# A two-layer decoder trunk on one core: an early exponent table, row maxima moved ahead, weight loads held, two more weight splits on Pool, and the gating mask a stage earlier

## The chip, the cores and the metric

The kernel runs on one core of a Trainium2 chip. That core has five engines that run side by side and meet only at semaphores: TensorE (PE, matrix multiplies and transposes), VectorE (DVE), ScalarE (ACT), GpSimd (POOL) and SyncE (SP, which here only starts transfers). The metric is device time in microseconds (us) of one launch; lower is better. Semaphore `hi_ready`, for instance, is a counter that ACT raises and that other engines wait on.

## The reference, cut to what matters

The program computes a decoder trunk of two layers on 256 positions of width 1024, all in float32. Each layer has three sub-blocks:

```
x = x + 1/2 * SwiGLU_a(RMSNorm(x))        # 1024 -> 2816 -> 1024
x = x + Mixer(RMSNorm(x))
x = x + 1/2 * SwiGLU_b(RMSNorm(x))
# layer 0 mixer: softmax attention (8 heads) beside a gated delta rule (8 heads), one output projection
# layer 1 mixer: u, v = gelu(h @ w_in); v = RMSNorm per group; gate = tril(w_s) @ v + b_s; (u*gate) @ w_out
```

In the delta rule the sequence is cut into four chunks of 64. Within a chunk a triangular system is solved; across chunks a state of 64 x 64 per head is carried (the scan): `v_new = u - w @ state`, `o = q_dec @ state + attn @ v_new`, `state = state * decay + k_tail^T @ v_new`. Its result is normalized per head (`rms_norm(o)`), multiplied with `silu(z)`, put beside the attention result, and goes through the output projection.

## The kernel before

The program is one straight list of instructions for each engine, written out by hand. It goes through six stages in order: feed-forward 0, the attention and delta-rule mixer ("the mixer", `ab`), feed-forward 1, feed-forward 2, the spatial gating mixer (`sg`), feed-forward 3. On each engine the order of the code is the order of execution; nothing reorders it, and an engine that waits holds up all that is behind it.

**Weights** come in units of 1 MB (128 partitions x 2048 words). `load_unit` on SP copies unit j into slot j mod 4 of the ring `raw`, once the slot's former unit has been split. The split makes two reduced-precision parts of a float32 weight: ACT copies `raw` to `whi` (`hi`, L466), and `wlo = raw - whi` is made by DVE (`lo`, L889) or by POOL (`pool_lo`, L426). `POOL_LO` lists the units that POOL splits; before the change these are units 12 to 15 of the mixer, its output projection. ACT may overwrite a slot of `whi` only when PE is done with the unit that is four before it (`unit_done`). PE multiplies with both parts, three products for each tile.

**The softmax part of the mixer.** ACT ends the short convolutions with `conv_silu(5)` (Silu table), then copies transposed channels out (`nt_out(5)`), then runs `exps(h)` for each head h, which needs the table of the exponential. `exps(h)` waits for `row_max(h)` on DVE (L1139 to L1141: the maximum over a row of scores, and the bias made of it), and PE transposes the exponentials (L1766) and computes the scores of head h + 2 (L1666) behind them. On DVE, between the first maxima, stand the head sums and the inverse root of the delta rule's q and k (`head_sums(1)` L1126, `rsqrt` L866 to L875, `head_norm` L1153), the copies of the summed log decays (L1161 and L1162, semaphore `gc_ready`) and the decay differences (`Dec`, L1184 and L1186), whose exponential ACT makes at L720 before it goes on to copy transposed heads (L686).

**The scan and what is behind it.** SP waits for `w_sums` 1, which PE raises when half of the matrices w are there, ahead of the scan, and then issues four loads, units 16 to 19 of the mixer's numbering, the first four of feed-forward 1. The scan is n = 0 to 3: DVE copies (L1265), PE L1918, L1924, L1906, L1910. Behind it DVE normalizes the result (`o_weighted` L1257 and L1259, `rsqrt`, and two products L1286 that raise `y_gdn`), while PE multiplies the attention half of the output projection (24 products, L1337 to L1339, `for t: for kk`). PE then waits for `y_gdn` 2, transposes (`y_transposes`, L1805) and goes on with the rest (`down`). ACT copies the transposes (`yT_hi`, L732), and splits units 16 and 17; DVE does `yT_lo` (L1222), its half of the split of units 16 and 17 (L889), and then updates X (`x_update`, L939, semaphore `x_updated`, four for each stage).

**The start of a stage** (`next_x`, `row_norm`, `spread_diag`): DVE computes 1 / rms of each row (`rsqrt`), multiplies it into an identity (L956, `r_diag`), and PE spreads it with two small products (L1480, `r_sums`) between its first weight products.

**The gating stage.** POOL waits for `x_updated` 16, the end of feed-forward 2, loads `v_norm_row` (1 MB, one row copied to all partitions) and `ws_raw` (the gating matrices, 512 KB), both through its own queue (L377), and multiplies `ws_raw` with a triangle (L450, `ws_masked`). PE transposes the result (L1972), ACT copies it to `wsT` (L826, `wsT_ready`) behind its splits. DVE waits for both loads (`sg_loaded` 32) before it scales v (L1309, `v_ready`), and splits two more units behind that; PE computes the first gates (L1958) when `v_ready` has reached 4.

Of the kernel before, what the change touches and what calls it, by code (L numbers as in the profile page):

```python
# [5 lines left out]
P = 128  # L6
D_MODEL, SEQ, D_FF = 1024, 256, 2816
NT = SEQ // P
# [5 lines left out]
HEADS = 8  # L14
# [59 lines left out]
def build_trunk(nc, x, positions, norm_w, w_gate, w_up, w_down, ab_in, q_norm, w_q_b, kv_norm, w_kv_b,  # L74
# [57 lines left out]
    u_ab = ab_units()  # L132
# [14 lines left out]
    with ctx:  # L147
# [5 lines left out]
        def S(name):  # L153
            if name not in sems:
                sems[name] = ctx.enter_context(nc.semaphore(name))
            return sems[name]
# [64 lines left out]
        v_norm_row = at(R0 + 2048, SGW)  # L221
        ws_raw = at(0, GROUPS, P)

# [87 lines left out]
        DT_SEED_BANKS = ((3, 6), (5, 2))  # L311
        POOL_LO = [u_ab + 12, u_ab + 13, u_ab + 14, u_ab + 15]
        SG_BANK = [(4, 5), (4, 5), (0, 1), (2, 3)]
# [5 lines left out]
        def _(sp_):  # L319
# [38 lines left out]
            if stop_after not in ("ffn0", "ab"):  # L358
                sp_.wait_ge(S("w_sums"), 1)
                ffn_loads(u_ffn[1])  # L360
                ffn_loads(u_ffn[2])
                for j in range(u_sg, u_sg + 24):
                    load_unit(j)
                ffn_loads(u_ffn[3])
# [10 lines left out]
        def _(pool):  # L375
            def load(dst, src, name):
                pool.dma_start(dst, src).then_inc(S(name), 16)  # L377
# [62 lines left out]
            pool_lo(u_ab + 14)  # L440
            pool_lo(u_ab + 15)

            if stop_after == "ab":
                return

            pool.wait_ge(S("x_updated"), 16)
            load(v_norm_row, bc(sg_norm, [P, SGW]), "sg_loaded")
            load(ws_raw, sg_ws[0].rearrange("g i j -> i g j"), "sg_loaded")
            pool.wait_ge(S("sg_loaded"), 32)
            nc.gpsimd.tensor_tensor(ws_raw, ws_raw, bc(const("tril128").unsqueeze(1), [P, GROUPS, P]),  # L450
                                    ALU.mult).then_inc(S("ws_masked"), 1)


        @block.scalar
        def _(act):
# [213 lines left out]
            conv_silu(5)  # L669
            nt_out(5)  # L670

# [16 lines left out]

            exps(0)
            exps(1)  # L690
            for h in range(HEADS):
# [85 lines left out]
            for n in range(4):  # L777
# [5 lines left out]
                if n >= 2:  # L783
                    o_squares(n - 2)
            yT_hi(4, 8)
            for j in range(16, 18):
                hi(b + j)
            next_x(2)
# [64 lines left out]
        def _(dve):  # L853
# [290 lines left out]
            row_max(0)  # L1144
            row_max(1)
            head_sums(1)
            dve.wait_ge(S("head_sums"), 2)
            both = qk_head_ss.rearrange("p a m -> p (a m)")
# [6 lines left out]
            head_norm(QKVn[1], 1, 1.0).then_inc(S("k_normed"), 1)  # L1155
            row_max(2)
            gcf, ekf = (a.rearrange("p t h -> p (t h)") for a in (gc, ek))
            dve.wait_ge(S("gc_sums"), 2)
            for c in range(2):
                r = slice(64 * c, 64 * c + 64)  # L1160
                link(nc.vector.tensor_copy(gcf[r, :], B[2 + c][r, 0:16]))  # L1161
                ins = TT(ekf[r, :], B[2 + c][r, 16:32], gcf[r, :], ALU.subtract)  # L1162
                if c == 0:
                    link(ins)
            ins.then_inc(S("gc_ready"), 1)

            m3 = lambda a: a.rearrange("p (m j) -> p m j", j=64)
# [7 lines left out]
            for h in range(HEADS):  # L1175
                if 0 < h < HEADS - 2:
                    row_max(h + 2)
# [109 lines left out]
            yT_lo(4, 8)  # L1287
            for j in range(16, 18):
                lo(b + j)
            next_x(2, [1.0, 1.0])  # L1290
# [42 lines left out]
        def _(pe):  # L1333
# [595 lines left out]
            pe.wait_ge(S("o_weighted"), 2)  # L1929
            for t in range(NT):  # L1930
                for kk in range(4):
                    wh, wl = slot(b + 12 + kk // 2)
# [81 lines left out]
```

## Time and profile before

| | us |
|---|---|
| median of 3 runs | 1094.08 |
| lowest, highest | 1093.31, 1097.67 |
| the profiled execution's own time | 1093.22 |
| its span (first to last instruction) | 1091.2 |
| outside the span (launch and end) | 2.0 |

| engine | busy us | share of span |
|---|---|---|
| PE | 1065.9 | 98% |
| DVE | 637.0 | 58% |
| ACT | 514.2 | 47% |
| POOL | 49.8 | 5% |

The mean granted TensorE clock is 0.998 of full speed. An engine's busy share says how much of the span it worked; a row of the timeline gives start, length, engine, line, operation, the tiles written and read and their shapes, and in square brackets the time that the engine sat idle just before, with the instruction that ended the wait. The chain of waits is the profile's own walk back from the last instruction to what released each step.

### The profile page before, as it was taken

How to read it: one execution, taken by the hardware profiler on the slowest of the kernel's cores; microseconds unless marked ns; L12 is line 12 of the kernel's file. 1: busy time of each engine (PE TensorE's matmuls, PEld its weight loads, DVE VectorE, ACT ScalarE, POOL GpSimd, SP SyncE). 2: the span in 40 equal slices, each digit the busy share in tenths (PEclk: the TensorE clock that was granted, in tenths of full speed). 3: DMA queues.
4: the chain of work that ended last, by engine and by line, in shares of the span. 5: the costliest groups of instructions: out<-in, count | busy, mean ns of one | idle time of the engine just before them, and what ended most of it. 6: DMA issues, size and time to landing. Idle time of an engine off the chain costs nothing.

```text
span 1091.2 us, 18956 instructions
## 1 busy us (share of the span) xinstructions
PE 1065.9 (98%) x8393; PEld 969.9 (89%) x8393; DVE 637.0 (58%) x783; ACT 514.2 (47%) x619; POOL 49.8 (5%) x32
## 2 busy tenths in 40 slices
PE   7999999999888999999999999999999999999998
PEld 7999988998777799998889999887788889999986
DVE  5756543699753675555457655435665547555542
ACT  6644433585673454443345444334665436444430
POOL 1000000110172000000000000001000000000000
PEclk9999999999999999999999999999999999999999
DMA  9856555253005276655538555554554465655531
GB/s 311 268 184 191 193 191 175 92 196 117 2 4 157 78 232 193 193 183 177 184 113 254 178 188 192 194 182 149 192 173 172 165 221 187 187 176 187 191 115 39
DMA packets 127194, 184.88 MB, mean 169 GB/s; under 512 B 4205, under 2 KB 101722, under 8 KB 126986
## 3 DMA queue, kind: packets, MB, share of 16 engines
q1 hardware_dynamic: 126368, 181.85, 51.3%
q0 software_dynamic: 448, 1.71, 0.5%
q8 instruction: 66, 1.08, 0.4%
q10 hardware_dynamic: 298, 0.12, 0.1%
q14 instruction: 14, 0.11, 0.0%
HBM read 182.62 MB, written 1.05 MB: 168 GB/s over the span
## 4 chain that ended last, share of the span: by engine, by line
PE 92%; DVE 4%; issue 2%; ACT 1%; DMA 0%; POOLq 0%; ACTq 0%; POOL 0%; DVEq 0%
PE banks L1337 21%; PE banks L1338 20%; PE banks L1339 20%; PE banks L1378 7%; PE banks L1382 7%; PE banks L1379 7%; PE banks L1735 1%; PE banks L1461 1%; PE banks L1462 1%; PE banks L1463 1%; PE banks L1425 1%; PE banks L1958 1%; DVE wlo L889 1%; DVE arena L1209 1%; DMA pos_rows<-in_positions 0%
## 5 line engine op out<-in xcount | busy, mean ns | idle before, releaser
L889 DVE TENSOR_TENSOR wlo<-raw,whi 128x2048 fp32r<-128x2048 f32 (+1 forms) x167 | 383.4, 2302 | 228.1 <-ACT whi L466 228.0
L466 ACT ACTIVATE whi<-raw 128x2048 fp32r<-128x2048 f32 (+1 forms) x171 | 324.1, 1908 | 382.0 <-PE banks L1339 241.8
L1337 PE MATMUL banks<-xTh,whi 128*128 128x256 f32 x1408 | 397.4, 282 | 1.0 <-DVE wlo L1011 0.9
L1338 PE MATMUL banks<-xTl,whi 128*128 128x256 f32 x1408 | 396.5, 282 | 0.0
L1339 PE MATMUL banks<-xTh,wlo 128*128 128x256 f32 x1408 | 396.5, 282 | 0.0
L1337 PEld LDWEIGHTS banks<-xTh,whi 128*128 128x128 f32 x1408 | 266.2, 189 | 1.7 <-issue 1.3
L1338 PEld LDWEIGHTS banks<-xTl,whi 128*128 128x128 f32 x1408 | 266.3, 189 | 0.0
L1339 PEld LDWEIGHTS banks<-xTh,wlo 128*128 128x128 f32 x1408 | 266.3, 189 | 0.0
L1378 PE MATMUL banks<-whi,hTh 128*128 128x512 f32 x336 | 133.4, 397 | 0.0
L1379 PE MATMUL banks<-wlo,hTh 128*128 128x512 f32 x336 | 132.3, 394 | 0.0
L1382 PE MATMUL banks<-whi,hTl 128*128 128x512 f32 x336 | 105.5, 395 | 0.0
L1378 PEld LDWEIGHTS banks<-whi,hTh 128*128 128x128 f32 x336 | 63.0, 188 | 15.5
L1382 PEld LDWEIGHTS banks<-whi,hTl 128*128 128x128 f32 x336 | 63.0, 187 | 15.4
L1379 PEld LDWEIGHTS banks<-wlo,hTh 128*128 128x128 f32 x336 | 63.0, 187 | 14.9
L1337 PE MATMUL banks<-whi,xTh 128*128 128x512 f32 (+1 forms) x160 | 64.0, 400 | 0.0
L1338 PE MATMUL banks<-wlo,xTh 128*128 128x512 f32 (+1 forms) x160 | 62.7, 392 | 0.0
L1339 PE MATMUL banks<-whi,xTl 128*128 128x512 f32 (+1 forms) x160 | 62.6, 391 | 0.0
L924 DVE TENSOR_TENSOR arena<-banks,arena 128x512 f32<-128x512 f32 x44 | 30.4, 690 | 53.6 <-PE banks L1339 53.6
L1337 PE MATMUL banks<-whi,hTh 128*128 128x512 f32 (+1 forms) x120 | 49.3, 411 | 0.0
L1339 PE MATMUL banks<-whi,hTl 128*128 128x512 f32 (+1 forms) x120 | 46.9, 391 | 0.0
L1338 PE MATMUL banks<-wlo,hTh 128*128 128x512 f32 (+1 forms) x120 | 46.9, 391 | 0.0
L915 DVE TENSOR_TENSOR arena<-banks,arena 128x512 f32<-128x512 f32 x44 | 30.3, 690 | 26.9 <-PE banks L1339 26.9
(249 smaller groups left out, 988.9 us busy)
## 6 DMA issues: line engine op xcount, KB each, us to landing
raw<-in_ffn_w_up SPq DMA_DIRECT2D x44, 1024.0 KB, 5.6
raw<-in_ffn_w_down SPq DMA_DIRECT2D x44, 1024.0 KB, 4.9
raw<-in_ffn_w_gate SPq DMA_DIRECT2D x43, 1024.0 KB, 5.4
raw<-in_sg_w_in SPq DMA_DIRECT2D x16, 1024.0 KB, 5.5
raw<-in_ab_w_in SPq DMA_DIRECT2D x8, 1024.0 KB, 5.2
raw<-in_sg_w_out SPq DMA_DIRECT2D x8, 1024.0 KB, 5.2
raw<-in_ab_w_out SPq DMA_DIRECT2D x4, 1024.0 KB, 4.8
raw<-in_ab_w_in SPq DMA_DIRECT2D x2, 832.0 KB, 4.4
```

What stands on the lines that cost most here:

```text
L466: A(whi[:, j % SLOTS, 0:kt * width], raw[:, j % SLOTS, 0:kt * width], ACT.Copy).then_inc(S("hi_ready"), 1)
L889: TT(wlo[:, j % SLOTS, 0:n], raw[:, j % SLOTS, 0:n], whi[:, j % SLOTS, 0:n].bitcast(f32), ALU.subtract).then_inc(S("lo_ready"), 1)
L915: TT(gate[:, c % 2, :].rearrange("p (b n) -> p b n", n=SEQ), B[PAIR_BANK[c][0]][:].rearrange("p (b n) -> p b n", n=SEQ), bc(r_row.unsqueez ...
L924: TT(prod[:, c % 2, :], B[PAIR_BANK[c][1]][:], gate[:, c % 2, :], ALU.mult).then_inc(S("prod_ready"), 1)
L1209: TT(LT_LEVEL[n][t].rearrange("p (m j) -> p m j", j=64), h3(LT, t), eight(f"level{LEVELS[n]}"), ALU.mult).then_inc(S("lt_level"), 1)
L1337: mm(out_ap, lh, rh, start=first, stop=False)
L1338: mm(out_ap, lh, rl, start=False, stop=False)
L1339: return mm(out_ap, ll, rh, start=False, stop=last)
L1378: mm(o, hTh[:, kk, tok], wh[:, k, c], start=kk == 0, stop=False)
L1379: mm(o, hTh[:, kk, tok], wl[:, k, c], start=False, stop=False)
L1382: last = mm(o, hTl[:, kk, tok], wh[:, k, c], start=False, stop=False)
L1425: last = transpose(B[X_BANK[k // 2]][:, 256 * (k % 2) + P * t:256 * (k % 2) + P * t + P], X[:, t, P * k:P * k + P], ident)
```

## The change

It has seven edits. One tiny exponential is put behind `conv_silu(5)`, and `nt_out(5)` moves behind `exps(0)`. On DVE the copies of the log decays and the maximum of head 2 move ahead of the inverse root, and the maximum of head 3 moves to just behind the norm of k. SP waits for `o_sums` 2, raised by PE in scan step n = 1, before the loads of feed-forward 1. Units 16 and 17 are split by POOL in place of DVE, ACT's part of unit 16 moves ahead of the last `yT_hi`, and PE's 24 products behind the scan run `for kk: for t`, so that unit 12 is released at half. The gating matrices are loaded and masked when `x_updated` reaches 8 (the end of the mixer), into another place of the arena (`R0 + 2912`); `v_norm_row` overlaps that place, and its load now waits for `wsT_ready` 2 as well.

```diff
-        ws_raw = at(0, GROUPS, P)
+        ws_raw = at(R0 + 2912, GROUPS, P)
...
-        POOL_LO = [u_ab + 12, u_ab + 13, u_ab + 14, u_ab + 15]
+        POOL_LO = [u_ab + i for i in range(12, 18)]
...
-                sp_.wait_ge(S("w_sums"), 1)
+                sp_.wait_ge(S("o_sums"), 2)
...
             pool_lo(u_ab + 15)
+            pool_lo(u_ab + 16)
+            pool_lo(u_ab + 17)
...
-            pool.wait_ge(S("x_updated"), 16)
-            load(v_norm_row, bc(sg_norm, [P, SGW]), "sg_loaded")
+            pool.wait_ge(S("x_updated"), 8)
             load(ws_raw, sg_ws[0].rearrange("g i j -> i g j"), "sg_loaded")
-            pool.wait_ge(S("sg_loaded"), 32)
+            pool.wait_ge(S("sg_loaded"), 16)
             nc.gpsimd.tensor_tensor(ws_raw, ws_raw, bc(const("tril128").unsqueeze(1), [P, GROUPS, P]),
                                     ALU.mult).then_inc(S("ws_masked"), 1)
+            pool.wait_ge(S("x_updated"), 16)
+            pool.wait_ge(S("wsT_ready"), 2)
+            load(v_norm_row, bc(sg_norm, [P, SGW]), "sg_loaded")
...
             conv_silu(5)
-            nt_out(5)
+            A(rope_tmp[:, 0, 0, 0:1], ones128[:, 0:1], ACT.Exp).then_inc(S("gate_exps"), 1)
...
             exps(0)
+            nt_out(5)
             exps(1)
...
+            hi(b + 16)
             yT_hi(4, 8)
-            for j in range(16, 18):
-                hi(b + j)
+            hi(b + 17)
...
             row_max(1)
-            head_sums(1)
-            dve.wait_ge(S("head_sums"), 2)
-            both = qk_head_ss.rearrange("p a m -> p (a m)")
-            link(rsqrt(both, both, 2 * M, 1.0))
...
-            head_norm(QKVn[1], 1, 1.0).then_inc(S("k_normed"), 1)
-            row_max(2)
             gcf, ekf = (a.rearrange("p t h -> p (t h)") for a in (gc, ek))
             dve.wait_ge(S("gc_sums"), 2)
...
             ins.then_inc(S("gc_ready"), 1)
+            head_sums(1)
+            row_max(2)
+            dve.wait_ge(S("head_sums"), 2)
+            both = qk_head_ss.rearrange("p a m -> p (a m)")
+            link(rsqrt(both, both, 2 * M, 1.0))
...
+            head_norm(QKVn[1], 1, 1.0).then_inc(S("k_normed"), 1)
+            row_max(3)
...
-                if 0 < h < HEADS - 2:
+                if 1 < h < HEADS - 2:
                     row_max(h + 2)
...
             yT_lo(4, 8)
-            for j in range(16, 18):
-                lo(b + j)
...
-            for t in range(NT):
-                for kk in range(4):
+            for kk in range(4):
+                for t in range(NT):
```

Two places show how the order on the engines moves. DVE in the softmax part of the mixer before, from the maximum of head 1 on; `banks` are the matmul results, `small` the small tiles, `128x3` the three maxima of a head:

```order
L1139 TENSOR_REDUCE small<-banks 128x3
L1140 TENSOR_TENSOR small<-small 128x1
L1141 TENSOR_TENSOR small<-small 128x2
L1126 TENSOR_REDUCE small<-arena 128x16
L866 TENSOR_SCALAR small<-small 128x32
```

And the same stretch of DVE after the change, where L1144 to L1146 are the maximum, L1155 and L1156 the copies of the decays, L1131 the head sums and L871 the first of the inverse root:

```order
L1144 TENSOR_REDUCE small<-banks 128x3
L1145 TENSOR_TENSOR small<-small 128x1
L1146 TENSOR_TENSOR small<-small 128x2
L1155 COPY small<-banks 64x16
L1156 TENSOR_TENSOR small<-banks,small 64x16
L1155 COPY small<-banks 64x16
L1156 TENSOR_TENSOR small<-banks,small 64x16
L1131 TENSOR_REDUCE small<-arena 128x16
L1144 TENSOR_REDUCE small<-banks 128x3
L1145 TENSOR_TENSOR small<-small 128x1
L1146 TENSOR_TENSOR small<-small 128x2
L871 TENSOR_SCALAR small<-small 128x32
```

Four copies and the third maximum stand ahead of the inverse root; all of them stood behind it. POOL from its splits to the end of its list before:

```order
L426 TENSOR_TENSOR wlo<-raw,whi 128x2048 x2
L377 DMA arena<-in_sg_v_norm 128x2048
L377 DMA arena<-in_sg_w_s 128x8x128
L450 TENSOR_TENSOR arena<-arena,C 128x1024
L147 UNCONDITIONAL_BRANCH
```

And after:

```order
L426 TENSOR_TENSOR wlo<-raw,whi 128x2048 x4
L377 DMA arena<-in_sg_w_s 128x8x128
L451 TENSOR_TENSOR arena<-arena,C 128x1024
L377 DMA arena<-in_sg_v_norm 128x2048
L147 UNCONDITIONAL_BRANCH
```

Two splits are added behind the two that were there, and the load of `v_norm_row` goes from the head of the gating's part to its end. ACT around the end of the scan, before and then after (first the squares of the scan's result, then `yT_hi`, with the splits `whi<-raw`):

```order
L773 ACTIVATE arena<-banks 128x4x64 x2
L732 ACTIVATE hTh<-banks 128x256 x4
L466 ACTIVATE whi<-raw 128x2048 x2
L481 ACTIVATE arena,small<-X 128x512 x2
```

```order
L778 ACTIVATE arena<-banks 128x4x64 x2
L470 ACTIVATE whi<-raw 128x2048
L737 ACTIVATE hTh<-banks 128x256 x4
L470 ACTIVATE whi<-raw 128x2048
L485 ACTIVATE arena,small<-X 128x512 x2
```

One of the two splits has moved ahead of the four copies.

## Rows read from the trace of the kernel before

**Rows 1.** Timeline of PE and ACT at the first exponentials (start us, us, engine, line).

```profile
279.19 0.55 PE L1766 MATMUL banks<-C,arena 128*128 128x128 f32 x3 [3.10 <-ACT arena L680]
276.74 1.28 ACT L678 ACT_TABLE_LOAD   x1
```

**Rows 2.** Stretch: us; busy us of PE, PEld, DVE, ACT, POOL; clock; DMA.

```profile
274.64:287.66 13.02, 9.41 (x73) 7.31 (x72) 11.96 (x35) 9.07 (x28) 0.00 (x0) 1.00 0.00 0
```

**Rows 3.** Timeline of ACT at the decay exponential.

```profile
287.70 1.06 ACT L720 ACTIVATE arena<-arena 128x1024 f32<-128x1024 f32 x1 [0.97 <-DVE arena L1186]
```

**Rows 4.** Chain of waits in order of time, the scan (start us, us, what).

```profile
344.31 1.44 issue
```

**Rows 5.** Timeline of DVE's copies in the scan, and of SP's loads.

```profile
340.38 0.42 DVE L1265 COPY arena<-banks 64x256 f32<-64x256 f32 x1 [6.24 <-PE banks L1893]
342.94 0.43 DVE L1265 COPY arena<-banks 64x256 f32<-64x256 f32 x1 [0.78 <-PE banks L1906]
347.91 0.41 DVE L1265 COPY arena<-banks 64x256 f32<-64x256 f32 x1 [3.19 <-PE banks L1906]
336.90 0.37 SPq L343 DMA_DIRECT2D raw<-in_ffn_w_gate  x1
```

**Rows 6.** Stretch in the scan, columns as in rows 2.

```profile
346.00:349.00 3.00, 3.00 (x56) 3.00 (x56) 0.75 (x2) 0.92 (x3) 0.00 (x0) 0.50 1.10 349
```

**Rows 7.** Timeline of PE, ACT and DVE behind the scan.

```profile
355.14 0.39 PE L1339 MATMUL banks<-whi,hTl 128*128 128x512 f32 x1
367.32 0.66 PE L1425 MATMUL banks<-C,X 128*128 128x128 f32 x4 [1.83 <-DVE X L939]
360.19 3.74 ACT L466 ACTIVATE whi<-raw 128x2048 fp32r<-128x2048 f32 x2
357.08 1.29 DVE L1286 TENSOR_TENSOR arena<-arena,small 128x512 f32<-128x512 f32 x2
362.17 4.49 DVE L889 TENSOR_TENSOR wlo<-raw,whi 128x2048 fp32r<-128x2048 f32 x2 [0.93 <-ACT whi L466]
```

**Rows 8.** Timeline of POOL, and of DVE beside it.

```profile
292.48 1.90 POOL L393 TENSOR_TENSOR arena<-arena,small 128x1024 f32<-128x1024 f32 x1
324.67 9.09 POOL L426 TENSOR_TENSOR wlo<-raw,whi 128x2048 fp32r<-128x2048 f32 x2
760.00 4.47 POOL L450 TENSOR_TENSOR arena<-arena,C 128x1024 f32<-128x1024 f32 x1 [5.47 <-DMA arena<-in_sg_w_s]
292.57 1.83 DVE L1141 TENSOR_TENSOR small<-small 128x2 f32<-128x2 f32 x1
```

**Rows 9.** Line L889 from 759 to 767 us: ns least/median/most, starts.

```profile
L889 DVE TENSOR_TENSOR wlo<-raw,whi x2: 2285/3376/4468, 760.0 to 762.2; 128x2048 fp32r<-128x2048 f32 x2
```

**Rows 10.** Timeline of DVE and PE at the start of feed-forward 1.

```profile
374.47 0.69 DVE L939 SCALAR_TENSOR_TENSOR X<-banks,X 128x512 f32<-128x512 f32 x1 [0.91 <-PE banks L1339]
379.98 0.15 DVE L900 TENSOR_TENSOR small<-small 128x2 f32<-128x2 f32 x1
382.60 0.48 DVE L956 TENSOR_SCALAR arena<-C,small 128x128 f32<-128x128 f32 x2
383.22 0.63 PE L1480 MATMUL banks<-arena,C 128*128 128x128 f32 x4
```

**Rows 11.** Timeline of PE, ACT and DVE in the gating stage.

```profile
764.53 1.09 PE L1972 MATMUL banks<-C,arena 128*128 128x128 f32 x8 [0.95 <-POOL arena L450]
776.66 1.89 PE L1958 MATMUL banks<-arena 128*128 128x256 f32 x8
770.14 1.05 ACT L826 ACTIVATE arena<-banks 128x512 f32<-128x512 f32 x2
769.13 1.67 DVE L1309 SCALAR_TENSOR_TENSOR arena<-arena,small 128x256 f32<-128x256 f32 x4
```

**Rows 12.** DMA issues on POOL's queue: KB each, us from issue to landing.

```profile
arena<-in_sg_v_norm POOLq DMA_DIRECT2D x1, 1024.0 KB, 5.3
arena<-in_sg_w_s POOLq DMA_DIRECT2D x1, 512.0 KB, 6.3
```

More of the change, by code:

```diff
@@ L1145, in _ @@
             row_max(1)
-            head_sums(1)
-            dve.wait_ge(S("head_sums"), 2)
-            both = qk_head_ss.rearrange("p a m -> p (a m)")
-            link(rsqrt(both, both, 2 * M, 1.0))
-            def head_norm(a, i, scale):
-                a3 = a.rearrange("p t (h d) -> p (t h) d", d=DK)
-                return STT(a3, a3, scale, bc(qk_head_ss[:, i, :].unsqueeze(2), [P, M, DK]), ALU.mult, ALU.mult)
-            head_norm(QKVn[1], 1, 1.0).then_inc(S("k_normed"), 1)
-            row_max(2)
             gcf, ekf = (a.rearrange("p t h -> p (t h)") for a in (gc, ek))
@@ L1165, in _, with head_norm @@
             ins.then_inc(S("gc_ready"), 1)
+            head_sums(1)
[3 more added lines that the diff above has]
+            link(rsqrt(both, both, 2 * M, 1.0))
+            def head_norm(a, i, scale):
+                a3 = a.rearrange("p t (h d) -> p (t h) d", d=DK)
+                return STT(a3, a3, scale, bc(qk_head_ss[:, i, :].unsqueeze(2), [P, M, DK]), ALU.mult, ALU.mult)
+            head_norm(QKVn[1], 1, 1.0).then_inc(S("k_normed"), 1)
+            row_max(3)
             m3 = lambda a: a.rearrange("p (m j) -> p m j", j=64)
```

## The prediction, made before the changed kernel had run

> **What bounds the kernel now.** PE works for 98% of the span, so a change can only gain where PE waits, or lose by making it wait. I read the chain of waits first, for the stretches that are not PE's; then the timeline of each engine around the edits; then the stretches, for the clock and for how full an engine is; last the transfers of POOL's queue. Five places matter, and all but the first are short:
>
> 1. Before the first exponentials PE sits idle 3.10 us, and a table load of 1.28 us on ACT lies in that wait [rows 1].
> 2. In the scan PE issues nothing for 1.44 us that any other engine explains [rows 4], and from 346 to 349 us its granted clock is 0.50, the 1.2 GHz level of the two [rows 6]. SP has started four weight loads at 336.90 [rows 5], and in the half-clock stretch DMA moves 349 GB/s [rows 6].
> 3. Behind the output projection PE waits 1.83 us for DVE's update of X [rows 7], and DVE has spent 4.49 us on the splits of units 16 and 17 just ahead of it [rows 7].
> 4. At the start of feed-forward 1 PE's spreading product stands at 383.22, right behind DVE's r_diag, which ends at 382.60 + 0.48 = 383.08 [rows 10]. There is 0.1 us of slack.
> 5. In the gating stage PE waits 0.95 us for POOL's mask [rows 11].
>
> **Exponent table and maxima: 0.** By themselves they let the first exponentials start when the first bias is ready, at about 275.6 and no longer at 278.04 (the end of the table load at 276.74 + 1.28), so PE's first transposes come some 2.3 us earlier. The question is what is late next. DVE is full from the first maximum to the decay differences: 11.96 us busy of 13.02 [rows 2], the rest being the small gaps between its chained instructions, and ACT waits at the end of that stretch for DVE's last one before it can make the decay exponential [rows 3]; ACT copies the transposed heads behind that, and PE needs these. The change moves DVE's work about inside this stretch: first maxima, four copies, head sums, third maximum, inverse root, norm, fourth maximum, norm, differences. The set is the same as before. So the decay exponential starts at 287.7 as before, PE waits behind it and not at 276, and 2.3 us go into another wait. I check that the third maximum doesn't stall DVE: the scores of head 2 are a few products behind the transposes, which would start at 276.8 and take 0.55 [rows 1]; I estimate them at 278.7, and DVE, with its copies and sums done first, arrives at about 278.6. Bounds: -2.3 us (all of it reaches the end), +0.5 (a short stall of DVE); I take 0, by the full engine.
>
> **Loads held to mid-scan: -2.8.** Scan step n = 0 takes 342.94 - 340.38 = 2.56 us, step n = 1 takes 347.91 - 342.94 = 4.97 [rows 5]. Without the stall it should be as short as its neighbour: 2.41 gained, in which the 1.44 and the first slow microseconds lie. The slow clock goes on for another microsecond behind 347.91 [rows 6]; I take 0.4 for it, from 1.1 us of matmuls at half rate, of which about a third is on the path. The cause that I assume is that PE's instructions are fetched by the same DMA engines, which were full. The loads now start at about 344.6, when the instructions for the rest of the scan are there, and the next block is wanted only behind 24 long products. Unit 16 is needed at 352.7 (new time), some 8 us after the issue; in rows of this trace a load of 1 MB lands 5.3 us after issue on POOL's queue [rows 12], so that it should be there. Bounds: -3.2, and 0 if the stall only moves to a later step.
>
> **Units 16 and 17 off DVE: -1.85 and +4.6.** Taking 4.49 us off DVE lets it update X when PE has finished the quarter, so that PE's wait of 1.83 us goes [rows 7]. The units themselves are not urgent: PE's spreading product at 383.22 [rows 10] stands amid its first products with units 16 and 17, 16 us behind that update, and one split takes POOL 9.09 / 2 = 4.54 us [rows 8].
>
> But POOL and DVE get into each other's way. At 292.57 a DVE product of two numbers per partition, from small tiles, took 1.83 us, and ended at 294.40; POOL's product, started at 292.48, ended at 294.38 [rows 8]. At 760.00 POOL's mask and DVE's splits ran together: DVE's two took 2285 and 4468 ns, POOL's 4.47 us [rows 8, 9]. The second DVE split, started at 762.2, ended at 766.7, and the only reading that fits all three is DVE 2.28, POOL 2.2, DVE 2.2, each alone: who waits gets the port when the other's instruction ends, even when the other has a next one ready. The Trainium skill's page "SBUF — State Buffer" (Who interferes with whom) says the same of a DVE instruction with two SBUF inputs beside a GpSimd one that reads SBUF, that one of them fully blocks, and not for one with a PSUM input. By that rule, the trace agrees.
>
> Now where POOL's split of unit 16 falls. ACT may start its part when PE has released unit 12. With `for kk: for t` that is the end of the twelfth product behind the scan, which in the old trace is the one at 355.14 with 0.39 us [rows 7]: 355.53. ACT takes 3.74 / 2, some 1.85 us: 357.4. POOL asks at 357.45. DVE at that time is in the first of the two products that end the norm, 357.08 to 357.72, with the second to follow [rows 7]; both read two SBUF operands. POOL gets in between, holds for 4.54 us, and the second product, which raises `y_gdn`, ends at 357.75 + 4.54 + 0.69 = 363.0 where it ended at 358.37. PE's transposes, all of them, wait for it: +4.6. The margin is 0.3 us, both chains start from the same last product of the scan and move together. Bounds: 0 (the request comes behind the second product), +5.3 (it comes ahead of both and the whole split stands in front). The split of unit 17 comes behind `yT_hi` and meets only updates with a PSUM input: nothing.
>
> **Mask a stage earlier: +1.9 at feed-forward 1.** `x_updated` 8 is the end of the update at 374.47 + 0.69 = 375.16 [rows 10]; POOL issues the load at about 375.4. It lands 6.3 us after issue when it stands behind the 1 MB load [rows 12]; alone, half as large, I put it at 4.3 (bounds 3 and 6.3). Then POOL's mask, 2.2 us without company (4.47 less DVE's 2.28 [rows 8, 9]), stands at 379.8 to 382.0. DVE's norm chain begins at 379.98 [rows 10] with products of two small tiles, the kind that was held at 292.57. It is held 1.0 to 2.2 us over the bounds of the landing, I take 2.0, and with 0.1 us of slack at place 4 PE waits 1.9. A landing within 2 us or behind 7.5 us would cost nothing.
>
> **Gating stage: +2.1.** The wait of 0.95 goes. But `v_norm_row` is now loaded only behind the copies to `wsT`, which end at 770.14 + 1.05 = 771.2 [rows 11], and takes 5.3 us [rows 12]: 776.6. DVE would have scaled v at 769.13 [rows 11]; it now starts at 776.6, and ends 1.67 us later, at 778.3. PE wants to start the gates at 776.66 at the latest [rows 11], 0.95 earlier without its former wait, and starts at 778.3: 1.65 later than before. Behind the gates (until 780.1) it wants unit b + 4 of the stage, and DVE's split of it, queued behind the scaling, ends at 778.3 + 2.25 = 780.5: 0.45 more. Later units have room. Bounds: 1.2 (landing 0.9 us faster, as no other load is under way) to 2.7.
>
> **Sum.** -2.8 - 1.85 + 4.6 + 1.9 + 2.1 = +3.95 us. The profiled execution took 1093.22 us (span 1091.2 and 2.0 around it): 1097.2. The median of the runs shown is 0.9 above it: 1098.0. I put 1097.6 between the two. What a measurement of this kernel can tell from no change is about 0.5%, 5.5 us: slower begins at 1099.6, faster at 1088.6.
>
> **Rivals.**
> - *POOL misses the norm's second product* (DVE keeps the port, or ACT's split ends 0.4 us later). For it: the margin of 0.3 us. Against: the pattern at 760. It takes away 4.6: 1093.
> - *The clock falls behind the long idle stretches: slower.* The forecast makes two long waits, 4.6 us before the transposes and some 2.6 us before the gates. The half-clock stretch of the old scan followed a wait of 1.44 us [rows 4, 6], against it stands that behind 3.10 us idle [rows 1] the clock stayed at 1.00 over the next 8 us [rows 2]. If it falls in the dense products behind both waits, and each time for as long as at 346 to 349, half of 3 us is lost twice: +3, 1100.6. It decides once both idle stretches lower the clock. The page "TensorE: Matmul & The Clock Gate" of the Trainium skill (Part 1) states that idleness takes the clock to the lower level; the trace shows one case for it and one against.
> - *The front gain reaches the end* (PE and ACT, not DVE, set the pace of the softmax part). For it: 3.10 us of PE idle. Against: rows 2 and 3. It gives -2.3: 1095.3.
> - *The mask runs clear of the norm.* For it: the landing of a lone 512 KB load is not in the trace. It gives -1.9: 1095.7.
>
> **Chances.** The forecast 0.44, POOL misses 0.18, clock 0.18, front gain 0.10, mask clear 0.10. Slower by over 0.5% holds most of the clock case (0.13) and the upper tail of the forecast (0.09): 0.22. Faster by over 0.5% needs three of the rivals together or a scan that gains more than I see: 0.09. The rest, 0.69, is within. The range goes from POOL missing, less 1.5, to the clock case: 1091.5 to 1101.
>
> **What will show it.** The first exponential should start near 275.7, and the decay exponential still near 287.7. Scan step n = 1 should take about 2.6 us and the clock there should read 1.00. The second of the two products L1291 should read about 5.2 us, and PE's wait before its transposes 4.7. The wait of 1.83 should be gone. POOL's mask should stand on DVE's inverse root of feed-forward 1, and PE wait about 1.9 us before `r_sums`. DVE should wait some 7 us for `v_norm_row`, PE about 2.6 before the first gates. I am wrong if the second product reads 0.69, if the decay exponential moves 2 us ahead, or if the stall of the scan comes back a step later.

## The result and the profile after

The changed kernel takes 1101.79 us (median of 14 runs, 1098.07 to 1104.32), the kernel before 1094.03 us beside it (14 runs, 1092.70 to 1100.66). The ratio is 1.0057, with a 95% interval of 1.0041 to 1.0072: slower by about 6.2 us, where the forecast had 1097.6, some 3.5 to 4 us above the kernel before. By the ratio, on the 1094.08 that the forecast started from, this is 1100.3, inside its range up to 1101; the median of 1101.79 itself lies above that range. Two executions behind this document (3689.89 us of the kernel before, 1491.17 us of the variant with the filler products) stand far outside all others and are left out of the ratios. The profiled execution took 1103.21 us (span 1101.4), 10.2 more in the span than the one of before.

I read the waits of PE first: it is busy for 97% of the span, so a loss must be a wait of PE or work of PE that takes longer. From the profile after, from 270 to 800 us (engine, line, what it waits for; us in total, times, longest):

```profile
PE banks L1808 <- DVE arena L1291: 4.4, 1, 4.4
PE banks L1961 <- DVE arena L1312: 3.2, 1, 3.2
PE banks L1703 <- ACT arena L690: 3.0, 1, 3.0
PE banks L1483 <- DVE arena L961: 2.0, 1, 2.0
```

Of before, the long ones were 3.10 at the first exponentials and 1.83 for X [rows 1, 7]. The four above stand where the forecast had put them. Then I went through the places. At the first exponentials, after, the timeline of ACT (start us, us, engine, line):

```profile
273.58 1.28 ACT L674 ACT_TABLE_LOAD   x1
275.56 0.46 ACT L682 ACTIVATE arena<-banks,small 128x128 f32<-128x128 f32 x1 [0.49 <-DVE small L1146]
287.51 1.06 ACT L725 ACTIVATE arena<-arena 128x1024 f32<-128x1024 f32 x1 [2.09 <-DVE arena L1191]
```

and of PE:

```profile
276.71 0.55 PE L1769 MATMUL banks<-C,arena 128*128 128x128 f32 x3 [0.69 <-ACT arena L684]
289.19 1.08 PE L1703 MATMUL banks<-C,arena 128*128 128x128 f32 x4 [3.00 <-ACT arena L690]
```

The table load lies ahead of the first maximum now, and PE's first transposes come 2.5 us earlier than in [rows 1]. But the decay exponential stands at 287.51, where it was at 287.70 [rows 3], and PE waits 3.00 us behind it in place of 3.10 ahead of it. The scan, DVE's copies:

```profile
342.04 0.42 DVE L1270 COPY arena<-banks 64x256 f32<-64x256 f32 x1 [6.23 <-PE banks L1896]
344.60 0.43 DVE L1270 COPY arena<-banks 64x256 f32<-64x256 f32 x1 [0.78 <-PE banks L1909]
347.17 0.42 DVE L1270 COPY arena<-banks 64x256 f32<-64x256 f32 x1 [0.78 <-PE banks L1909]
349.72 0.43 DVE L1270 COPY arena<-banks 64x256 f32<-64x256 f32 x1 [0.78 <-PE banks L1909]
```

Every step takes 2.56 us. The one of 4.97 in [rows 5] is gone, and with it the issue gap of [rows 4] (a stretch in which PE waits for nothing that the profile shows). Behind the scan, the timeline of ACT, DVE, POOL and PE:

```profile
354.50 1.91 ACT L470 ACTIVATE whi<-raw 128x2048 fp32r<-128x2048 f32 x1 [2.39 <-PE banks L1342]
355.95 5.60 DVE L1291 TENSOR_TENSOR arena<-arena,small 128x512 f32<-128x512 f32 x2
356.49 4.52 POOL L426 TENSOR_TENSOR wlo<-raw,whi 128x2048 fp32r<-128x2048 f32 x1 [20.78 <-ACT whi L470]
361.61 1.97 PE L1808 MATMUL banks<-C,arena 128*128 128x128 f32 x8 [4.41 <-DVE arena L1291]
370.37 0.60 PE L1428 MATMUL banks<-C,X 128*128 128x128 f32 x4
```

POOL's split starts in the first of DVE's two products, and the pair takes 5.60 us where it took 1.29 [rows 7]; the wait of 1.83 us for X has gone from the last row. The start of feed-forward 1, the timeline of POOL, DVE and PE:

```profile
378.46 0.94 POOL L377 DMA_DIRECT2D arena<-in_sg_w_s  x1 [7.68 <-DVE X L944]
383.62 2.40 POOL L451 TENSOR_TENSOR arena<-arena,C 128x1024 f32<-128x1024 f32 x1 [4.22 <-DMA arena<-in_sg_w_s]
383.64 2.41 DVE L875 TENSOR_SCALAR small<-small 128x2 int32<-128x2 int32 x1
388.38 0.71 PE L1483 MATMUL banks<-arena,C 128*128 128x128 f32 x4 [2.00 <-DVE arena L961]
```

POOL's mask and a DVE instruction on two numbers per partition start within 0.02 us and end together; its neighbours on DVE take 0.16 to 0.17. The gating stage, the timeline of PE, POOL and DVE:

```profile
768.64 1.04 PE L1975 MATMUL banks<-C,arena 128*128 128x128 f32 x8
776.98 0.59 POOL L377 DMA_DIRECT2D arena<-in_sg_v_norm  x1 [390.97 <-ACT arena L831]
782.39 1.67 DVE L1312 SCALAR_TENSOR_TENSOR arena<-arena,small 128x256 f32<-128x256 f32 x4 [8.07 <-DMA arena<-in_sg_v_norm]
784.12 3.78 PE L1961 MATMUL banks<-arena 128*128 128x256 f32 x8 [3.24 <-DVE arena L1312]
```

The wait for the mask [rows 11] is gone from the first row, and the last has one of 3.24. Its product also takes 3.78 us where it took 1.89 [rows 11]: exactly twice. That made me read the clock, in three stretches of after (columns as in [rows 2]):

```profile
288.00:294.00 6.00, 4.81 (x23) 4.84 (x24) 2.49 (x6) 3.40 (x9) 4.03 (x2) 0.50 0.01 3
360.00:366.00 6.00, 4.39 (x15) 3.73 (x16) 3.07 (x5) 3.04 (x5) 1.01 (x1) 0.50 0.60 192
783.00:789.00 6.00, 4.88 (x12) 3.87 (x13) 5.93 (x9) 4.90 (x10) 0.00 (x0) 0.50 0.27 51
```

Behind three of the four waits PE works at the 1.2 GHz level; behind the one of 2.00 us the clock stays at 1.00. Following one instruction after another through both traces, the difference (after less before) grows so, in us:

| up to | difference | step | what it is |
|---|---|---|---|
| head transposes behind the decay exponential | -0.2 | | front |
| products of the chunks, 292.45 before | +2.4 | +2.6 | half clock, first stretch |
| first scan copy | +1.7 | -0.7 | not told apart |
| last scan copy | -1.1 | -2.8 | hold of the loads |
| transposes of y, 358.43 before | +3.2 | +4.3 | port taken by POOL's split |
| first product of the next quarter, 362.53 before | +5.1 | +1.9 | half clock, second stretch |
| spreading product, 367.32 before | +3.1 | -2.0 | wait for X gone |
| spreading product of feed-forward 1 | +5.2 | +2.1 | POOL's mask on the inverse root |
| gating, first transposes | +4.1 | -1.1 | wait for the mask gone |
| first gates | +7.5 | +3.4 | late `v_norm_row` |
| second gates | +10.2 | +2.7 | half clock, third stretch |
| end | +10.2 | 0 | |

The three clock steps are 7.2 in this execution; without them the difference is +3.0. (The kernel before has a half-clock stretch of its own in its scan [rows 6], which is part of the -2.8.) This execution is above its own median, and the one of before was a little under its own, so the two medians lie closer than the two spans.

### The profile page after: what moved, and what is told of

It is laid out like the page before. It is cut to its first block, busy times and chain, and to the rows that moved or that the text cites. A ratio compares the mean times of both kernels' runs of the same rounds, so it can differ in the third digit from the quotient of the medians.

```text
span 1101.4 us, 18958 instructions
## 1 busy us (share of the span) xinstructions
PE 1070.9 (97%) x8393; PEld 973.4 (88%) x8393; DVE 635.6 (58%) x781; ACT 514.7 (47%) x620; POOL 57.1 (5%) x34
## 4 chain that ended last, share of the span: by engine, by line
PE 91%; DVE 4%; ACT 1%; DMA 1%; issue 1%; SPq 0%; DVEq 0%; ACTq 0%; POOLq 0%
PE banks L1340 20%; PE banks L1342 20%; PE banks L1341 20%; PE banks L1381 7%; PE banks L1385 7%; PE banks L1382 7%; PE banks L1738 1%; PE banks L1464 1%; PE banks L1466 1%; PE banks L1465 1%; PE banks L1961 1%; DMA raw<-in_ffn_w_up 1%; PE banks L1428 1%; DVE arena L1214 1%; DVE arena L1291 1%
## 5 line engine op out<-in xcount | busy, mean ns | idle before, releaser
L894 DVE TENSOR_TENSOR wlo<-raw,whi 128x2048 fp32r<-128x2048 f32 (+1 forms) x165 | 376.8, 2289 | 228.5 <-ACT whi L470 228.4
```

The lines of the kernel that those rows point to most:

```text
L894: TT(wlo[:, j % SLOTS, 0:n], raw[:, j % SLOTS, 0:n], whi[:, j % SLOTS, 0:n].bitcast(f32), ALU.subtract).then_inc(S("lo_ready"), 1)
```

## The experiments

The times are medians. Each ratio is to the kernel before on the same chip, whose median was 1094.2 to 1094.8 us, with its 95% interval.

**Each part alone.** Theory A: the parts cost and bring what the forecast says, and add up; the clock comes on top behind the long waits. Rival B: one of the parts is worth something quite different (the front's gain is real and hidden by something else, or the whole loss is the clock's).

The front, as in the change, and nothing else:

```diff
-            nt_out(5)
+            A(rope_tmp[:, 0, 0, 0:1], ones128[:, 0:1], ACT.Exp).then_inc(S("gate_exps"), 1)
...
             exps(0)
+            nt_out(5)
...
```

> The kernel before with the early exponent table and the moved row maxima alone. My forecast's theory (DVE is full there, nothing reaches the end): 0 us, decay exponential at about 287.5. Clock theory (PE now sits idle 3.0 us ahead of the head transposes, and the granted clock may fall to 0.50 for about 7 us behind it, as in the profile of the changed kernel): +2 us in the executions where it falls, 0 in the others, so a median of +0.5 to +2 and a wider spread. Rival (the gain at the first exponentials reaches the end): -2.3.

1095.35 us, ratio 1.0005 (0.9987 to 1.0023), so that a gain of 2.3 is excluded. PE in the profile of this kernel:

```profile
276.51 0.55 PE L1767 MATMUL banks<-C,arena 128*128 128x128 f32 x3 [0.68 <-ACT arena L680]
288.99 0.63 PE L1701 MATMUL banks<-C,arena 128*128 128x128 f32 x4 [3.00 <-ACT arena L686]
```

The first wait is 0.68 and no longer 3.10, the second 3.00. The gain becomes a wait 12 us on, and no change of the time can be measured. The first four products behind that wait still run at full clock (0.63 us), but from 290 to 293 us the granted clock is 0.50 here too.

The hold of the loads alone:

```diff
-                sp_.wait_ge(S("w_sums"), 1)
+                sp_.wait_ge(S("o_sums"), 2)
```

> The kernel before with the weight loads held to scan step n = 1 alone. Theory (the fetch of instructions stood behind the loads): -2.8 us, scan step n = 1 at 2.6 us, no half clock in the scan. Rival (the stall moves to a later step, or unit 16 comes too late): between -1 and +1, with an issue gap or a wait for raw in the profile.

1092.28 us, ratio 0.9986 (0.9972 to 1.0000). The four copies stand 2.56, 2.57 and 2.56 us apart, as in the kernel after, without an issue gap above 0.2 us. About 1.5 us of gain by the ratio, 2.8 forecast; the interval reaches from 0 to 3.1.

The Pool splits alone, with the order of the 24 products:

```diff
-        POOL_LO = [u_ab + 12, u_ab + 13, u_ab + 14, u_ab + 15]
+        POOL_LO = [u_ab + i for i in range(12, 18)]
...
+            pool_lo(u_ab + 16)
+            pool_lo(u_ab + 17)
...
+            hi(b + 16)
             yT_hi(4, 8)
-            for j in range(16, 18):
-                hi(b + j)
+            hi(b + 17)
...
-            for t in range(NT):
-                for kk in range(4):
+            for kk in range(4):
+                for t in range(NT):
```

> The kernel before with units 16 and 17 split by Pool alone (ACT's part of 16 ahead of the last copies, products in the order kk, t). Port theory: PE waits about 4.4 us before the transposes, second product of the norm about 5 us long, the wait of 1.83 for X gone: +2.6 us, and +2 more where the clock falls behind that wait: +2.6 to +4.6. Rival (Pool and DVE do not exclude each other here): -1.8.

1092.09 us, ratio 0.9982 (0.9963 to 1.0001). This is a miss: I had expected it to be slower. The timeline of PE, ACT, DVE and POOL:

```profile
352.67 0.50 PE L1338 MATMUL banks<-wlo,hTh 128*128 128x512 f32 x1 [0.56 <-issue]
355.61 1.92 ACT L468 ACTIVATE whi<-raw 128x2048 fp32r<-128x2048 f32 x1 [3.22 <-PE banks L1339]
356.23 1.29 DVE L1288 TENSOR_TENSOR arena<-arena,small 128x512 f32<-128x512 f32 x2
357.60 9.18 POOL L426 TENSOR_TENSOR wlo<-raw,whi 128x2048 fp32r<-128x2048 f32 x2 [23.99 <-ACT whi L468]
```

There is no collision. ACT's split ends at 357.53 and DVE's products at 357.52, so POOL asks just as DVE is done. ACT starts 0.62 us ahead of DVE's products here, and 1.45 ahead in the kernel after (354.50 and 355.95). What holds it back is the first row, an issue gap of PE in the second product behind the scan: DVE's chain hangs on the scan and had its last result, ACT's hangs on the twelfth product and slips. Such a gap was not in the kernel with the hold. It is in three of the four profiles without the hold (0.55 with the front alone, 0.56 here and with the mask alone), but not in the profile of before, whose PE runs on behind the scan. So the miss is that of this execution; that the split costs nothing in every execution of this kernel isn't shown.

The mask and `v_norm_row` alone:

```diff
-        ws_raw = at(0, GROUPS, P)
+        ws_raw = at(R0 + 2912, GROUPS, P)
...
-            pool.wait_ge(S("x_updated"), 16)
-            load(v_norm_row, bc(sg_norm, [P, SGW]), "sg_loaded")
+            pool.wait_ge(S("x_updated"), 8)
...
+            pool.wait_ge(S("x_updated"), 16)
+            pool.wait_ge(S("wsT_ready"), 2)
+            load(v_norm_row, bc(sg_norm, [P, SGW]), "sg_loaded")
```

> The kernel before with the gating matrices loaded and masked at the end of the mixer, and the row of norm weights loaded behind the copies to wsT, alone. Theory: +2.0 at the start of feed-forward 1 (mask on DVE's inverse root), and +2.2 at the gates (the row lands late), +2.7 more where the clock falls behind PE's wait at the gates: +4.2 to +6.9. Rival (only the row's lateness costs): +2.2.

1100.96 us (median of 6), ratio 1.0060 (1.0037 to 1.0083), and this part alone is as slow as the whole change, within the intervals. PE:

```profile
386.69 0.71 PE L1482 MATMUL banks<-arena,C 128*128 128x128 f32 x4 [1.91 <-DVE arena L958]
783.62 3.68 PE L1960 MATMUL banks<-arena 128*128 128x256 f32 x8 [2.90 <-DVE arena L1311]
```

and the clock behind both (columns as in [rows 2]):

```profile
387.00:391.00 4.00, 4.00 (x24) 4.00 (x23) 3.97 (x3) 2.18 (x2) 0.00 (x0) 0.59 0.18 45
783.00:787.00 4.00, 3.38 (x9) 2.73 (x9) 4.00 (x4) 3.40 (x9) 0.00 (x0) 0.59 0.05 9
```

The waits of the forecast are there, 4.0 in its sum, and the rest of 6.6 us (0.0060 of 1094) is about what half clock behind them costs: in this profile the difference to the kernel before grows by 1.6 us behind the first wait and by 1.8 behind the second.

**Do the parts add up?** By their ratios the four give +0.5, -1.5, -2.0 and +6.6 us, together +3.6; the change has +6.2. The intervals, of 1.5 to 2.5 us on each part, are too wide to tell these two sums apart. The traces do: the third has no collision, the change has one of 4.3 us. They name the pair: hold and Pool splits. So I ran the two together, the sum of the two diffs above.

> The kernel before with the held loads and the two Pool splits, nothing else. With the split edit alone PE had an issue gap of 0.56 us behind the scan (amid the loads), Pool asked at 357.60 and came behind the norm's second product (which ended at 357.5), and nothing was lost. Theory of a margin: without the loads in the way that gap is not there, Pool comes in ahead of the second product, the two products read 5.6 us together, PE waits about 4.4 us before the transposes: -2.8 - 1.85 + 4.4 = 0, and +2 where the clock falls behind it: 0 to +2. Rival (no collision without the other edits either): -4.6.

1094.80 us, ratio 1.0000 (0.9984 to 1.0015), where the two apart would give 0.9968; the difference is about as large as the uncertainty of the three ratios together, so that here too the traces carry the reading. The timeline:

```profile
353.81 5.61 DVE L1288 TENSOR_TENSOR arena<-arena,small 128x512 f32<-128x512 f32 x2
354.36 4.52 POOL L426 TENSOR_TENSOR wlo<-raw,whi 128x2048 fp32r<-128x2048 f32 x1 [20.30 <-ACT whi L468]
359.48 1.51 PE L1805 MATMUL banks<-C,arena 128*128 128x128 f32 x8 [4.42 <-DVE arena L1288]
```

The collision is back, 5.61 us for the pair. The hold takes away the gap that had kept the splits harmless in the profile without it, and what it gains goes there.

**The collision taken away**, in the kernel after:

```diff
             pool_lo(u_ab + 15)
+            pool.wait_ge(S("y_gdn"), 2)
             pool_lo(u_ab + 16)
```

> The changed kernel with one wait more: Pool starts its split of unit 16 only when y_gdn has reached 2. Port theory: the two products of the norm read 1.29 us, PE's wait of 4.4 us before the transposes is gone, and with it the half clock behind it: -4.3 to -6.3 against the changed kernel, 1095.5 to 1097.5. Rival (the late split of 16 and 17 makes PE wait for wlo later): less than -3.

1094.62 us, ratio 1.0000 (0.9988 to 1.0012), against 1.0057 for the kernel after: 6.2 us from one wait on POOL. The products take 1.29 us again and POOL's two splits start at 356.69. 4.3 is the collision itself, the rest is about the 1.9 of the clock step behind it. The three other waits stay, at 3.1, 3.0 and 1.9.

**The mask taken away from the norm**, in the kernel after: a place in the arena that `v_norm_row` doesn't overlap, so that its load need not wait for the copies, and the mask itself behind a later semaphore of feed-forward 1.

```diff
-        ws_raw = at(R0 + 2912, GROUPS, P)
+        ws_raw = at(R0 + 7168, GROUPS, P)
...
+            pool.wait_ge(S("gate_scaled"), 16)
...
             pool.wait_ge(S("x_updated"), 16)
-            pool.wait_ge(S("wsT_ready"), 2)
```

> The changed kernel with the gating matrices in a place of the arena that v_norm_row does not overlap: its load waits for x_updated 16 alone again, and Pool's mask waits until the fifth gate of feed-forward 1 has been scaled, off the row norm. Theory: PE's 2.0 us before r_sums and 3.2 us before the gates go, with the half clock behind the latter (2 us), and PE's former 0.95 us before the transposes of the masks stays gone: -5.2 to -7.5 against the changed kernel, 1094.3 to 1096.6. Rival (only one of the two waits belongs to this edit): -2 to -3.

1094.12 us, ratio 0.9991 (0.9979 to 1.0003): 7.2 us less than the kernel after. The waits of 3.2 and 2.0 are gone, the 4.4 before the transposes stays; POOL masks at 428.67, amid products, and issues `v_norm_row` at 754.36.

**Is it idleness that lowers the clock?** The pair above (hold and splits) has the wait of 4.42 and behind it half clock. I kept PE busy in that wait by 16 products into a bank that nobody reads then; they add nothing to the output.

```diff
+            wh, wl = slot(b + 13)
+            for i in range(16):
+                mm(B[5][:], hTh[:, i % 4, 0:P], wh[:, i % 2, 512:1024], start=True, stop=True)
             pe.wait_ge(S("y_gdn"), 2)
```

> The kernel with held loads and Pool splits (which waits 4.4 us before the transposes), with 16 products added ahead of that wait; they go to a bank whose content is not used, so nothing that is computed changes. They fill some 3.7 us of the wait and make PE no later. Clock theory: the granted clock stays at 1.00 behind the wait, -1 to -2 us against the same kernel without them (1094.8): 1093 to 1094. Rival (the clock falls for another reason than idleness): no difference, half clock from 360 us on as without them.

1093.67 us, ratio 0.9978 (0.9961 to 0.9995), against 1094.80 and 1.0000. The stretch from 361 to 363 us, first without the filler:

```profile
361.00:363.00 2.00, 2.00 (x6) 1.52 (x6) 1.37 (x4) 1.98 (x3) 0.00 (x0) 0.50 1.07 380
```

then with it, and with PE's transposes ahead of it:

```profile
361.00:363.00 2.00, 1.87 (x12) 1.53 (x13) 0.65 (x2) 1.34 (x5) 0.00 (x0) 1.00 0.66 170
```

```profile
360.97 1.09 PE L1805 MATMUL banks<-C,arena 128*128 128x128 f32 x8 [0.77 <-DVE arena L1288]
```

DVE's pair is as long as before (5.70 us), yet the eight transposes take 1.09 us and not 1.51, and the clock reads 1.00. That is one profile, and one in which the clock stayed up by chance would look the same; but the wait of 4.4 us without the filler has half clock behind it in all three profiles that have it (the kernel after, the one with its mask taken away from the norm, and this pair), and the 11 executions with the filler that the ratio uses have mean clocks of 0.996 to 1.000, against 0.993 to 0.998 in the 12 without, on another chip. So in one place, with the collision unchanged, the clock followed the idle time. The rule cited in the forecast, from the Trainium skill's page "TensorE: Matmul & The Clock Gate" (Part 1), says so too; by that, the trace agrees here. In the time it is 1.1 us by the medians and 2.4 by the ratios, and the intervals overlap; the size rests on the traces.

**A version that keeps the gains:** the hold, Pool's splits behind `y_gdn`, and the mask as in the clean version, without the front.

> The kernel before with held loads, the two Pool splits behind y_gdn, and the mask as in the kernel with its own place; without the exponent table and the moved maxima. Theory: -2.8 - 1.85 - 0.95 - 2.2 (DVE's split no longer blocked, off the path: 0) = -5.6 against the kernel before: 1088.5 to 1089.5. Rival (the gains overlap or come back as a wait later): -3 or less.

1087.72 us (median of 6), ratio 0.9935 (0.9919 to 0.9951): 0.65% faster than before, and 13 us under the kernel after by the ratios (14 by the medians). That is 7.1 us of gain where 5.6 had been expected; the interval reaches from 5.4 to 8.9. PE's only wait above 1.6 us in this part of the program is the old one at the first exponentials:

```profile
PE banks L1769 <- ACT arena L685: 3.1, 1, 3.1
```

Behind this same wait, behind which the clock stayed at 1.00 in the profile of before, the clock is low here (columns as in [rows 2]):

```profile
280.00:286.00 6.00, 5.96 (x22) 4.12 (x23) 5.11 (x16) 4.43 (x17) 0.00 (x0) 0.50 0.00 0
```

And the same with the front's edits as well:

> The fastest version (1087.7) with the exponent table and the moved maxima as well: what the first part of the change is worth beside the mended rest. Theory (DVE is full; PE's idle stretch of 3.1 us ahead of the exponentials becomes one of 3.0 us ahead of the head transposes, with the same chance of half clock behind it): -0.5 to +1, 1087.2 to 1088.7. Rival (the early start pays once the rest is in order): 1085.4.

1088.47 us (median of 6), ratio 0.9936 (0.9911 to 0.9962). The wait has moved again, with nothing gained:

```profile
PE banks L1704 <- ACT arena L691: 3.0, 1, 3.0
```

**How often a wait lowers the clock.** The experiments leave twelve profiles, with before and after, and they hold the same few waits again and again:

| PE waits before | length, us | profiles that have it | half clock behind it |
|---|---|---|---|
| the first exponentials | 3.10 | 7 | 4 |
| the head transposes (front moved) | 3.0 | 5 | 5 |
| the transposes of y | 4.4 | 3 | 3 |
| the first gates | 2.9 to 3.2 | 3 | 3 |
| the spreading product of feed-forward 1 | 1.9 to 2.0 | 3 | 1 |
| the spreading product, for X | 1.8 | 4 | 0 |
| transposes ahead of the scan, near 310 us | 1.6 | 12 | 2 |

The stretches lasted from about 3 to about 7 us. The profile of before, from which the forecast was made, is one of the three in seven that kept the full clock behind its wait of 3.10.

## Why the prediction came out as it did

**Exponent table and maxima, 0: right.** The decay exponential moved by 0.2 us, and alone and on top of the best version the part changes nothing that can be measured. The reading of [rows 2] carried it: after, DVE is busy 11.87 of 12.89 us of the same stretch. The rival that the gain reaches the end falls. What I left out is the clock behind the moved wait: half clock followed it in all five profiles that have it, and this execution lost 2.6 us there; behind the old wait it followed in four of seven.

**Loads held, -2.8: right for this pair of profiles, large for most.** The steps of the scan are equal and the trace gives -2.8; alone it measures -1.5, with an interval that reaches to -3.1. The step n = 1 took 4.97 us in the profile that the forecast read, but 4.38, 3.85 and 3.85 in the three others without the hold (front alone, Pool splits alone, mask alone), and only the first had half clock behind its gap. From the first copy to the last the hold is thus worth 2.8, 1.8, 1.3 and 1.3 us, and in the last three a gap of 0.55 us behind the scan goes with it.

That PE's instructions come late beside the loads was the forecast's assumption. The traces bear it out. They record transfers of a kind called instruction, of 16 KB each, beside those of the loads. From 339 to 342 us, in the profile of before:

```profile
q1 hardware_dynamic: 1104, 1.11, 108.6%
```

and in that of the hold alone:

```profile
q8 instruction: 1, 0.02, 2.1%
```

With the loads under way no instruction transfer starts in these 3 us, in any of the four profiles without the hold; with the hold there is one in seven of the eight (in the eighth, the version that keeps the gains, the scan stands later in time). The gap goes when the loads start later, and a second one shows where they start early (1.1 us in the scan and 0.56 behind it in the profile of the Pool splits alone). What holds the transfer up beside the loads isn't shown.

**Units 16 and 17, -1.85 and +4.6: measured -2.0 and +4.3.** POOL asked at 356.49, 0.54 us into a pair of 1.29, and got the port between the two products. The mechanism and the arithmetic were right, but one premise that I didn't see as one was the supply of PE behind the scan, which the hold makes sure of. The forecast priced the two edits in separate sentences; without it, in three of four profiles, an issue gap stands there, and in the one with the splits it moves ACT's split by 0.83 us against DVE's products (1.45 less 0.62), more than the margin of 0.3 us that I gave, and the split costs nothing. The Trainium skill's page "SBUF — State Buffer" (Who interferes with whom) has that issue order, and not the kind of operation, decides who blocks. By that, the trace agrees: the split asked at 356.49 stood ahead of the second product, which had to wait, and cost 4.3 us; asked 0.08 behind both, it costs nothing.

**Mask a stage earlier, +1.9: measured 2.1 in the table.** The load landed 5.1 us after issue, where I had put 4.3, and was issued at 378.46, 3 us later than reckoned, since all that stands ahead had shifted. Both the mask and the norm shifted with it, so that they still met. What was held was not a product of two small tiles, on which the forecast had reasoned, but an instruction with one input. The rival that the mask runs clear falls.

**Gating, +2.1: measured -1.1 and +3.4, +2.3 in sum.** The single landing of 5.3 us is as in [rows 12]. POOL issued the load at 776.98, 0.56 behind the end of ACT's copies (775.36 and 1.06), where the forecast had it at once; the 0.45 that the forecast added for DVE's split behind the gates doesn't show, since PE goes on without a wait behind them, though at half clock. The two nearly cancel. The terms of the sum thus come to +3.9 (-2.8, -2.0, +4.3, +2.1, +2.3) beside the forecast's +3.95; the table's other -0.9 stands in the front and ahead of the scan.

**The clock: the mis-sized term.** The forecast had the sum without it, and named it as the rival for the slower side, with two stretches and +3. It happened together with the forecast's own waits, behind three of them (the forecast had counted two and not the one moved by the front), and the profiled execution lost 2.6, 1.9 and 2.7 us. The sum +3.95 with +3 is +6.95, beside 6.2 by the ratio. The step that failed, in a forecast whose range held by the ratio, is thus the choice to leave it out, on the strength of one wait of 3.10 us behind which the clock stayed at 1.00 [rows 2]. One execution was too little for that: of the same kernel before, executions on these chips went from 1091.0 us at a mean clock of 0.998 to 1099.9 at 0.990, and the profiled one was near the good end. For the same reason the 7.2 us are not what the clock adds to the medians, since the kernel before loses time to it as well: the mean clocks of the 14 executions after center at 0.992 to 0.993, those of before, in the rounds of the experiments, at 0.995. By subtraction, 6.2 less the 3.0 of the waits, some 3 us are left for it; that is an estimate from one pair of profiles. The price of one such stretch was low as well: 1.5 us, half of the 3 us of [rows 6], where PE works for some 4 to 6 us in the stretches of after, and they cost 1.9 to 2.7.

What stays open: the -0.7 between the chunk products and the scan, and why one wait lowers the clock and another of the same length doesn't. The counts of profiles in the table are too few for a chance.

## What to carry to other kernels

When PE is busy for 97% of a span, a removed wait is worth only what is not late next: look for the engine that is full in that stretch, and for what PE does behind the place to which the wait moves. Price every long wait that a change creates together with the half-clock stretch that may follow, and judge the clock from several executions, not from one. And where two edits touch the same 2 us, ask what each is worth with the other in place: here the one that gained took away a delay that had kept the other harmless in its own profile, and one semaphore wait on POOL was worth 6.2 us.

## What the hardware showed that I had not expected

- Behind waits of 3.00, 4.41 and 3.24 us PE worked for some 4 to 6 us at 1.2 GHz, and behind one of 2.00 it didn't in the kernel after, but it did behind 1.91 with the mask alone (0.59 from 387 to 391 us). Behind 3.10 it stayed at 2.4 GHz in the profile of before and in two others, and fell in four. The length of the wait alone doesn't settle it.
- The kernel's own spread follows it: after, 14 executions go from 1098.07 us at a mean clock of 0.997 to 1104.32 at 0.991.
- A DVE TENSOR_SCALAR on 2 integers per partition, with one SBUF input, was held for 2.41 us by POOL's product. The instruction of the same kind and shape just ahead of it takes 0.16. Not only the products with two inputs are at risk.
- A POOL load of 512 KB alone landed in 5.1 us, hardly sooner than one of 1 MB (5.3).
